# Running the first four output tiles behind each RMS norm on unnormalised x in a two-layer diffusion backbone

## The reference

```
def rms_norm(x, g):
    y = xf * lax.rsqrt(jnp.mean(xf * xf, axis=-1, keepdims=True) + EPS)
    return (y * g.astype(jnp.float32)).astype(x.dtype)
def modulated(x, mod, gains, j):
    return rms_norm(x, gains[j]) * (1.0 + mod[:, :, 3 * j + 1]) + mod[:, :, 3 * j]
def swiglu(h, w_in, w_out):
    g, u = jnp.split(h @ w_in, 2, axis=-1)
    return (jax.nn.silu(g) * u) @ w_out
def half_ffn(x, mod, gains, j, w_in, w_out):
    return x + FFN_RES * mod[:, :, 3 * j + 2] * swiglu(modulated(x, mod, gains, j), w_in, w_out)
```

## Time and profile before

| | |
|---|---|
| median of 3 runs | 1666.97 us (1665.94 to 1670.01) |
| profiled execution, first to last instruction | 1668.0 us |
| PE busy | 1537.1 us, 92% |
| DVE busy | 1192.3 us, 71% |
| ACT busy | 624.6 us, 37% |
| POOL busy | 329.4 us, 20% |
| mean granted TensorE clock, share of full | 0.955 |
| moved by DMA | 256.96 MB, mean 154 GB/s |

### The profile page before, as it was taken

One profiled execution on the slowest core, in us unless ns is written; L12 is line 12 of the kernel. 1 busy time (PEld: TensorE's weight loads), 2 busy tenths in 40 slices (PEclk: granted clock), 3 DMA queues, 4 the chain that ended last, 5 costly groups with the idle time before them and its releaser, 6 DMA issues.

```text
span 1668.0 us, 24331 instructions
## 1 busy us (share of the span) xinstructions
PE 1537.1 (92%) x8554; PEld 1500.3 (90%) x8554; DVE 1192.3 (71%) x1745; ACT 624.6 (37%) x876; POOL 329.4 (20%) x377
## 2 busy tenths in 40 slices
PE   6899999999636899999989999998989899999997
PEld 6899999989626899999989999997869889999997
...
DMA packets 67074, 256.96 MB, mean 154 GB/s; under 512 B 7472, under 2 KB 8496, under 8 KB 66640
## 3 DMA queue, kind: packets, MB, share of 16 engines
...
q10 hardware_dynamic: 912, 1.65, 0.3%
...
HBM read 253.68 MB, written 2.63 MB: 154 GB/s over the span
## 4 chain that ended last, share of the span: by engine, by line
PE 73%; DVE 15%; issue 5%; POOL 3%; ACT 3%; DMA 2%; SPq 0%; DVEq 0%; ACTq 0%; POOLq 0%
PE bank L531 21%; PE bank L533 21%; PE bank L532 20%; DVE wide L1110 4%; DVE wide L1113 3%; PE bank L569 2%; PE bank L570 2%; PE bank L573 2%; DVE w_lo_sb L1091 1%; DVE gv L1410 1%; PE wide L712 1%; DMA ada_raw<-in_ada_w 1%; DMA x<-in_x 1%; ACT w_hi_sb L814 1%; DVE x L1252 1%
## 5 line engine op out<-in xcount | busy, mean ns | idle before, releaser
L1091 DVE TENSOR_TENSOR w_lo_sb<-raw,w_hi_sb 128x1024 fp32r<-128x1024 f32 (+2 forms) x304 | 428.4, 1410 | 172.9 <-ACT w_hi_sb L814 167.5
L531 PE MATMUL bank<-h_hi,w_hi_sb 128*128 128x384 f32 x1620 | 546.3, 337 | 3.0 <-DVEq L1530 3.0
L533 PE MATMUL bank<-h_hi,w_lo_sb 128*128 128x384 f32 x1620 | 544.9, 336 | 0.0
L532 PE MATMUL bank<-h_lo,w_hi_sb 128*128 128x384 f32 x1620 | 544.9, 336 | 0.0
L814 ACT ACTIVATE w_hi_sb<-raw 128x1024 fp32r<-128x1024 f32 (+2 forms) x304 | 343.3, 1133 | 536.7 <-PE bank L533 528.6
L531 PEld LDWEIGHTS bank<-h_hi,w_hi_sb 128*128 128x128 f32 x1620 | 305.1, 188 | 4.9 <-DVEq L1530 3.2
L532 PEld LDWEIGHTS bank<-h_lo,w_hi_sb 128*128 128x128 f32 x1620 | 305.1, 188 | 0.1
L533 PEld LDWEIGHTS bank<-h_hi,w_lo_sb 128*128 128x128 f32 x1620 | 305.0, 188 | 0.0
L531 PE MATMUL bank<-a_hi,w_hi_sb 128*128 128x384 f32 x704 | 237.1, 337 | 3.3 <-DVEq L1271 1.8
L533 PE MATMUL bank<-a_hi,w_lo_sb 128*128 128x384 f32 x704 | 236.6, 336 | 0.0
L532 PE MATMUL bank<-a_lo,w_hi_sb 128*128 128x384 f32 x704 | 236.6, 336 | 0.0
...
## 6 DMA issues: line engine op xcount, KB each, us to landing
raw<-in_ffn_in SPq DMA_DIRECT2D x176, 512.0 KB, 3.4
ada_raw<-in_ada_w POOLq DMA_DIRECT2D x128, 512.0 KB, 3.6
...
raw<-in_rg_in SPq DMA_DIRECT2D x20, 512.0 KB, 3.4
...
raw<-in_gla_qk SPq DMA_DIRECT2D x8, 512.0 KB, 4.0
raw<-in_gla_v SPq DMA_DIRECT2D x8, 512.0 KB, 3.4
```

Source lines behind the costliest of these rows:

```text
L531: pe.matmul(out, w_hi_sb[:, slot, w], hi[k], start=start and j == 0, stop=False)
L532: pe.matmul(out, w_hi_sb[:, slot, w], lo[k], start=False, stop=False)
L533: last = pe.matmul(out, w_lo_sb[:, slot, w], hi[k], start=False, stop=stop and j == len(ks) - 1)
L1091: V.tensor_tensor(w_lo_sb[:, s, 0:w], raw[:, s, 0:w], w_hi_sb[:, s, 0:w].bitcast(F32), ALU.subtract).then_inc(w_split, 1)
```

## The change

For the norms 1 to 5, PE runs the first four tiles of the next phase on gain·x, which needs no row factor, and with two more columns that hold the shift of either token group (386 columns). DVE multiplies each of the four banks by r when it empties it (`early_scale`); the columns' product, W·shift (also times a factor of one), is added by the operation that follows. Chunk by chunk behind each update of x, ACT makes h_hi from gain·x (`early_hi`) and DVE h_lo (`early_lo`). The fifth tile is the first to read the true h, chunk by chunk (`first_tile`). On DVE and ACT the chunks of true h are made four before and four between the eviction of the early tiles.

```
+            def early_tiles(q, base):
+                for b in range(RING):
+                    pe.wait_ge(w_split, base + b + 1)
+                two_banks = q in (1, 3, 4)
+                for k in range(EARLY):
+                    pe.wait_ge(xg_ready, DC * (q - 1) + k + 1)
...
+                    if k == 0:
+                        norm_sums(q)
+                    if k == 2:
+                        norm_spread(q)
+                pe.wait_ge(xg_ready, DC * q)
+                for b in range(RING):
+                    tile(bank[b][:, 0:HX], b, range(EARLY, DC), *xg_chunks, False, True, EARLY).then_inc(w_used, 1)
...
+            def early_lo(q, m):
+                dve.wait_ge(xghi_ready, DC * (q - 1) + m + 1)
...
+                for t0, n, g in GROUPS:
+                    last = V.scalar_tensor_tensor(col_major(h_lo[:, m, t0:t0 + n], q, n),
+                                                  row_major(x[:, m, t0:t0 + n], q, n), gain[:, q, m, g:g + 1],
+                                                  col_major(h_hi[:, m, t0:t0 + n].bitcast(F32), q, n),
+                                                  ALU.mult, ALU.subtract)
+                last.then_inc(xg_ready, 1)
...
+                def early_turn():
+                    early_scale(q, base, 0)
+                    ahead(base)
+                    norm_lo(q, (4, 5))
+                    early_scale(q, base, 1)
+                    ahead(base + 1)
+                    norm_lo(q, (6, 7))
+                    early_scale(q, base, 2)
+                    early_scale(q, base, 3)
+                    ahead(base + 2)
+                    early_product(0)
+                    ahead(base + 3)
+                    early_product(1)
...
                     if b:
                         ahead(base + b)
+                    if b % 2 and q < 6:
+                        early_lo(q, b // 2)
```

The modulation blocks move too. The first two tile pairs of ffn_in1 and ffn_in2 now reduce none, so that four are left behind the last pair where two were; and the RG-LRU's eight are all in rg_gates, two per block:

```
+                per = 2
+                first = 1 if f else 0
+                left = FC - 2 - per * first
...
-                        for b in range(2, ADA_IN - (FC - 2)):
-                            ada_at(ada + FC - 2, b)
+                        for b in range(2, ADA_IN - left):
+                            ada_at(ada + left, b)
...
-                ada_at(n_ada, b)
+                for k in range(ADA_RING):
+                    ada_at(n_ada, ADA_RING * b + k)
```

More of the change, by code:

```diff
@@ L621, in _ @@
             ffn(0, 0)
-            norm(1)
-            one_tile_blocks("rg_in", h_chunks, range(DC), hhi_ready, h_ready, DC)
+            early_blocks("rg_in", 1)
             base = BASE["rg_gates"]
```

383 lines of the change are left out of this document (276 added, 107 removed).

## The result

| | before | changed |
|---|---|---|
| median | 1667.38 us (1665.94 to 1670.01) | 1728.62 us (1724.44 to 1730.74) |
| profiled span | 1668.0 us | 1722.8 us |
| PE busy | 1537.1 us | 1555.0 us |
| DVE busy | 1192.3 us | 1235.1 us |
| mean granted TensorE clock | 0.955 | 0.952 |

The changed kernel is slower: ratio 1.0361, 95% interval 1.0343 to 1.0379. The forecast was slower too, but 1700 us with an upper end of 1716. Against the earlier trace rows the span grew by 54.8 us where the sum had 33.6.

A forecast was written before the change was run, and what follows sets the result against it. VectorE was taken to lead the stretch before three of five norms, TensorE idling there. Norms 1 to 5 added 5.7, 2.8, 11.5, 11.2 and 2.4: +33.6 us, a time of 1700 us, 2% slower, range 1674 to 1716.

The forecast's parts named there:

- The low products in the mixers: In rg_out and gla_out, 0.78 us each: hidden in rg_out, 3.0 us later in gla_out after its idle.
- The wait for a late load: In ffn_in2's tail: a 3.85 us wait falls away, so four modulation blocks cost only 3.1 us.
- its own prices: Ends of the unknown prices (low products, rg_gates blocks, spread, clock) together make about 1676 to 1718.
- the step from span to median: Profiled span 1668.0 us lies 1.0 us above the runs' median, so the difference in span is added to that median.
- What bounds: VectorE leads the stretch before three of five norms; TensorE idles 18.7 us before column sums, 7.0 before spreads.
- Rival (b): VectorE is on time at every norm, the clock stays full: 17 us less, 1650 us; chance 0.12.
- rival (a): VectorE has more slack; new products and rg_gates' second blocks cost nothing: 1667 us; chance 0.10.
- S at norm 1: S, when the fourth weight split ends behind ffn_out0's last update, comes 5.7 us later: low products and shift columns.
- From S to T: From last weight split to five tiles done: 26.1 us at full clock, 28.5 after long idle, 31.0 at norm 4.
- half of it at 2 and 5: At norms 2 and 5 TensorE idles some 2.5 to 5 us, so half of the 2.4 us clock cost.
- Rival (c): Each new product in the ffn_outs also collides with GpSimd: 21 x 0.81 = 17 us more, 1717 us; chance 0.10.
- The blocks: Moved modulation reductions on VectorE: 6.8 us behind ffn_in1, 3.1 behind ffn_in2, 10 in rg_gates, where second blocks are uncovered.

The follow-up runs named there:

- before_rows386: Kernel before, with rows of 386 instead of 384 columns in h_hi and h_lo, 384 used: 1681.32 us, ratio 1.0078.
- after_small_squares: Changed kernel, GpSimd forming squares and sums of the second to seventh chunk on 2 columns in rg_out and gla_out: 1716.35 us, ratio 1.0297.
- combo: Changed kernel, early tiles one after the other, 96 bytes ahead of a_hi, modulation blocks moved in both ffn_ins and from rg_gates: 1664.54 us, 0.9982 of the kernel before.

## Why the prediction was right, and where it failed

The direction was right and the size was not: 33.6 us forecast, 54.8 in the profiled execution. The steps that failed are four. The low products in the mixers were to cost 0.78 us and to hide in rg_out; they took 2.14 beside GpSimd. The wait for a late load was to fall away behind ffn_in2; it stayed at 3.72. The half clock was taken as 1.2 us at norms 2 and 5; it cost 4.7. And the place of the data had no term at all. The stated range, 1674 to 1716, also lies 2 us below the 1676 to 1718 that its own prices gave, of which the step from span to median explains 1.

**What bounds, right.** VectorE leads the stretch ahead of norms 1, 3 and 4, and no early matmul ran before the last split. Rival (b), in which VectorE is on time, did not happen; of rival (a) one part did, since the product took the reduction's place in the collision, but it still cost 0.6 us and not nothing. That S at norm 1 moved by 5.6 us against 5.7 is partly luck. The products gave 4.3 of the 5.7, and 1.0 came from before ffn_out0, whose first update starts at 260.00 instead of 259.04 behind the slower matmuls of ffn_in0; 0.4 is the step from the split's end to the matmul. The last update ahead of norm 3 stood 3.6 us behind TensorE's last matmul, not some 8, since TensorE was late as well.

**From S to T, right in its steps, off in the clock.** 26.9 and 27.4 us at norms 1 and 3 against 28.5, and 29.6 against 31.0 at norm 4: VectorE's row of factor, products and evictions made the fifth tile wait 1.65 us (2.46 at norm 4), not 2.5. At norms 2 and 5 it was 30.8 against 27.3. The step "half of it at 2 and 5" failed: TensorE idled 6.9 and 8.75 us there, not some 2.5 to 5, and half clock lasted some 12 us. At norm 2 that length is chance, and at norm 1 its absence is: other executions of the same instructions show either length. Why is open.

**The low products, mis-sized in the mixers.** In the ffn_outs a pair on VectorE rose from 10.53 to 11.14, 0.6 instead of 0.78. In the mixers the sum priced a product at 0.78 and let rg_out hide it, because it compared tile times (5.2 us of TensorE) and not the start, four tiles behind; it cost 2.14 beside GpSimd's squares. Rival (c) had this very collision with 0.81 a product, but in the ffn_outs, where rows 4 showed it. In the mixers GpSimd has a square and an addition for every tile, and in the ffn_outs for every pair of 11 us. S came 3.5 us later than forecast at norm 2 and 5.3 at norm 5. after_small_squares gives 12 us for the collision, part of it by the clock.

**The blocks.** In rg_gates 10 us forecast, 11 measured when the second blocks were taken out. Behind ffn_in1 6.8 forecast; VectorE's first update, at 774.9 and now 798.4, stood 13.8 us behind TensorE's short wait for the last a_lo (761.1) and now stands 21.4 us behind it (777.0), 7.6 more. Behind ffn_in2 3.1 was forecast and 6.7 measured, by the same reading (1064.4 - 1047.0 = 17.4, 1098.8 - 1074.7 = 24.1): "the wait of 3.85 us for a later load falls away" failed, since that load is issued only after VectorE's own block two back, and so moves with VectorE. TensorE's stop after the second pair of ffn_out1 was forecast and came, 4.70 us.

**What no term held.** Slower matmuls by where the rows start. "Rows of 386 columns" stood in the diff as a matter of memory alone. before_rows386 gives 12 to 13 us in the old kernel. In the changed one the part that better places give back is 1 to 3 us, hard to tell from none, as long as VectorE leads the ffn_outs. The rest is not split off by any run: by the spacings it is 1.8 us in each ffn_in (960 matmuls x 1.9 ns) and most of the 3.5 us behind norm 5. In combo, where the starts on a are good, the updates of ffn_out3 come every 11.44 us again.

These effects overlap: taken out one at a time the low products of the ffn_outs, squares, second blocks and two tail blocks give 10.5, 12, 11 and 5.6 us, and the tile order alone 40, because each shortens the same late start of VectorE or fills it. Each also changes how long the half clock lasts, by up to 4 us a norm.
